# Query tiles of unequal width alternate in the self-attention sections of a two-block kernel

## What is computed

```python
QUERY_BLOCK = 128
def masked_probs(s, mask, sink=None):      # softmax over the keys that the mask leaves
    ...
def swa_mixer(q, k, v, pos, sinks):        # window of 128 keys: a block sees itself and the one before
    ...
def nsa_mixer(...):                        # compressed keys, selected blocks, window of 512
    ...
        return (g[..., 0:1] * o_cmp + g[..., 1:2] * o_sel + g[..., 2:3] * o_win)
def mla_mixer(...):                        # causal, scores are the sum of two products
        s = (jnp.einsum('bqhd,bkhd->bhqk', qn, k_nope)
             + jnp.einsum('bqhd,bkd->bhqk', qp, k_pe)).astype(jnp.float32) * scale
        p = masked_probs(s, kpos <= t)
        return jnp.einsum('bhqk,bkhd->bqhd', p.astype(v.dtype), v)
```

## Time and profile before

| | us |
|---|---|
| median of 3 runs | 3393.14 |
| the runs | 3391.33 to 3394.71 |
| the profiled execution | 3396.96 |
| its span (first to last instruction) | 3395.2 |
| PE busy in the span | 3277.1 (97%) |
| DVE busy | 1471.4 (43%) |
| ACT busy | 684.9 (20%) |
| section 0, 1, 2 of the first layer start near | 1136, 1309, 1555 |
| section 0, 1, 2 of the second layer start near | 2276, 2447, 2694 |

### The profile page before, as it was taken

How to read it: one execution, slowest core, us unless ns; L and a number is a source line. 1 busy time by engine, 2 the same in 40 slices (tenths; PEclk the granted TensorE clock), 3 DMA queues, 4 the chain that set the end, 5 groups by cost and what they waited for, 6 DMA issues and landing times.

```text
span 3395.2 us, 36971 instructions
## 1 busy us (share of the span) xinstructions
PE 3277.1 (97%) x14532; PEld 2105.3 (62%) x14532; DVE 1471.4 (43%) x2922; ACT 684.9 (20%) x1422; POOL 148.8 (4%) x106
## 2 busy tenths in 40 slices
PE   8999998999999999999999999999999999999998
PEld 3446345433433575765865888857467478568887
DVE  2352114212113646736644554346484375255533
ACT  2132111000002415413121000033361231210000
POOL 4400010000000100000000000000000000000000
PEclk9998998999999999999999999999999999999999
DMA  6110634999996121120221222221202112222221
GB/s 247 40 66 26 225 125 165 409 409 409 408 409 261 40 88 49 37 76 32 75 87 62 87 87 101 94 73 58 75 8 87 57 57 97 71 75 87 87 93 68
DMA packets 118635, 433.42 MB, mean 128 GB/s; under 512 B 13120, under 2 KB 13888, under 8 KB 117696
## 3 DMA queue, kind: packets, MB, share of 16 engines
q1 hardware_dynamic: 114768, 417.91, 33.0%
q10 hardware_dynamic: 3696, 13.16, 1.0%
HBM read 427.87 MB, written 3.15 MB: 127 GB/s over the span
## 4 chain that ended last, share of the span: by engine, by line
PE 85%; DVE 6%; DMA 4%; ACT 2%; issue 1%; DVEq 1%; POOL 0%; ACTq 0%; SPq 0%
PE bank L605 83%; DMA ring<-in_stream 2%; PE bank L1171 2%; DMA arena<-in_stream 2%; DVE arena L2088 1%; DVE arena L2113 1%; DVE arena L2110 1%; DVEq L2087 0%; ACT arena L1469 0%; DVE bank L2079 0%; ACT arena L1432 0%; DVE arena L2138 0%; DVE arena L2105 0%; DVE bank L2075 0%; ACT arena L1502 0%
## 5 line engine op out<-in xcount | busy, mean ns | idle before, releaser
L605 PE MATMUL bank<-arena 128*128 128x256 f32 (+14 forms) x5448 | 954.8, 389 | 36.3 <-ACT arena L1469 9.1
L605 PEld LDWEIGHTS bank<-arena 128*128 128x128 f32 (+4 forms) x5448 | 610.1, 173 | 324.8 <-issue 184.1
L605 PE MATMUL bank<-h,ring 128*128 128x256 f32 (+1 forms) x2000 | 672.8, 491 | 3.0 <-ACT rstd L1512 1.7
L605 PEld LDWEIGHTS bank<-h,ring 128*128 128x128 f32 x2000 | 384.2, 193 | 263.0 <-issue 230.8
L605 PE MATMUL bank<-arena,ring 128*128 128x256 f32 (+2 forms) x1888 | 513.5, 426 | 5.0 <-DVE y L1793 3.5
L605 PEld LDWEIGHTS bank<-arena,ring 128*128 128x128 f32 (+1 forms) x1888 | 336.8, 186 | 165.7 <-issue 122.4
L605 PE MATMUL bank<-ring,arena 128*64 128x512 f32 (+2 forms) x1184 | 282.7, 603 | 22.3 <-ACT arena L1315 11.5
L605 PE MATMUL bank<-y,ring 128*128 128x256 f32 (+1 forms) x800 | 253.9, 473 | 1.5 <-DVE y L1874 1.5
L605 PE MATMUL bank<-y,arena 128*128 128x256 f32 (+1 forms) x1032 | 231.8, 381 | 0.0
L1652 POOL TENSOR_TENSOR sq<-sq 128x512 f32<-128x512 f32 (+1 forms) x62 | 78.9, 1273 | 3179.8 <-ACT sq L1296 3179.8
L605 PEld LDWEIGHTS bank<-ring,arena 128*64 128x64 f32 (+2 forms) x1184 | 90.6, 139 | 203.9 <-issue 157.3
(11 more groups left out here) (299 smaller groups left out, 2445.1 us busy)
## 6 DMA issues: line engine op xcount, KB each, us to landing
ring<-in_stream SPq DMA_DIRECT2D x629, 512.0 KB, 4.6
arena<-in_stream SPq DMA_DIRECT2D x168, 512.0 KB, 12.8
x<-in_xT ACTq DMA_DIRECT2D x1, 2048.0 KB, 11.0
arena<-in_memT ACTq DMA_DIRECT2D x2, 1024.0 KB, 6.3
outT<-h ACTq DMA_DIRECT2D x8, 256.0 KB, 2.1
arena<-in_ctxT ACTq DMA_DIRECT2D x1, 1024.0 KB, 5.8
y<-in_inv ACTq DMA_DIRECT2D x1, 1024.0 KB, 4.8
memory_kv<-arena ACTq DMA_DIRECT2D x1, 1024.0 KB, 3.9
```

The lines of the kernel that those rows point to most:

```text
L605: ins = pe.matmul(out, lhsT, rhs, start=start, stop=stop, skip_group_check=loose)
```

## The change

Before the units get their numbers, the list is put in a new order for sections 0 to 2: first the units of qt 3 and qt 0 in turn (wide, narrow, wide, narrow, ...), then those of qt 2 and qt 1 in turn. The order inside a tile stays, and so do section 3 and all instructions of a unit. The number og of a tile follows the new order of completion: qt 3, 0, 2, 1. The two tiles that alternate have output banks 6 and 7.

```diff
@@ -523,9 +523,13 @@
+            def of(sec, qt):
+                return [u for u in out if u["sec"] == sec and u["qt"] == qt]
+            out = [u for sec in range(3) for wide, narrow in ((3, 0), (2, 1)) for two in zip(of(sec, wide), of(sec, narrow))
+                   for u in two] + [u for u in out if u["sec"] == 3]
             for i, u in enumerate(out):
                 u["n"] = i
-                u["og"] = 4 * u["sec"] + (TT - 1 - u["qt"] if u["sec"] < 3 else u["qt"])
+                u["og"] = 4 * u["sec"] + ((1, 3, 2, 0)[u["qt"]] if u["sec"] < 3 else u["qt"])
             return out
```

## The result

The changed kernel took 3429.45 us (median of four runs, 3422.01 to 3440.99) against 3392.68 us for the kernel before (3391.33 to 3394.71): a ratio of 1.0111, interval 1.0090 to 1.0133. The forecast was 3402 us with a range of 3396 to 3414. The direction is right, the size is not: 37 us were lost where 9 were forecast. Another thing is new. The four runs of the kernel before lie 3.4 us apart, those of the changed kernel 19.

The account below looks back on a forecast made before the run. PE was taken to bound wide units and DVE narrow ones, in a two-unit loop. Sections with drain +12.4, clock behind sections -6.5 and clock at starts +2.5 made +8.4 us: 3402 us, range 3396 to 3414.

Parts of the forecast that it names:

- What bounds the kernel, and the loop: PE bounds wide units, DVE narrow ones; a PE-DVE chain makes a (512, 128) pair 5.07 us instead of 4.66.
- Rival 1: Mixing works in the alternating sections: a pair takes only DVE's 4.37 us instead of 4.66, total 3376 us; chance 0.05.
- Section 1, +4.4: Section 1 of each layer: eight (512, 128) pairs lose 3.3 us, eight (384, 256) pairs 1.1, together 4.4.
- Section 0, +0.5: Section 0 of each layer: its first four pairs, widths 256 and 128, lose 0.14 us each, 0.5 together.
- Section 2, +1.3: Section 2 of each layer: 0.25 us for each of four pairs, 1.0, and 0.3 for the drain.
- 384, 256 stays bound by PE: 0: Section 2's pairs of 384 and 256 keys stay bound by PE and lose 0 us.
- Drain and the falls behind a section, -6.5: Section ends: last PV about 0.5 us later; half-clock falls behind five sections go, 1.3 us each, -6.5.
- The clock at a start: Section starts: with the second unit narrow, half clock may come or last longer; +2.5 us, bounds 0 and +15.
- rival 3: Half clock spreads at section starts, 20 us instead of 10, costing 3 to 5 us a place: 3407 to 3417; chance 0.20.
- Rival 2: Behind the sections, the ends stay slow and the five half-clock falls stay: 3408.5 us; chance 0.12.

Follow-up runs that it names:

- e8: Kernel before with only section 1 reordered, two wide units then two narrow ones in turn: 3414.86 us, ratio 1.0066.
- e16: The changed kernel run again with nothing altered, compared with the kernel before: 3419.18 us, ratio 1.0080.
- e13: Changed kernel with section 2 opening on two wide units (3 3 0 3 0 3 0 0), then tiles 2 and 1 in turn: 3404.90 us.
- e11: Kernel before with whole tiles from narrowest to widest (0, 1, 2, 3) in sections 0 to 2, no alternation: 3411.99 us, ratio 1.0053.
- e17: Kernel before with only section 2 reordered: 3 3 0 3 0 3 0 0, then tiles 2 and 1 in turn: 3394.40 us, ratio 1.0003.
- e15: Kernel before with only section 0 alternating, tiles 3 and 0, then 2 and 1: 3400.02 us, ratio 1.0018.

## Why the prediction was right or wrong

- **What bounds the kernel, and the loop** (right). The pair takes 5.07 us, term by term as added up. e8 gives the same reading with another order. Rival 1, the mix works, is out: 4.37 was its pair. The Trainium skill, Perfetto Trace Analysis, section Optimization Strategy, says that interleaving regimes with different bounds may improve performance; the premise held here and the result didn't: no order that mixed tiles was faster than whole tiles.
- **Section 1, +4.4** (nearly right). +5.8 and +5.2 in the first profile, +5.6 and +5.2 in e16. The (512, 128) pairs lose what was forecast, the (384, 256) pairs 0.04 each and not 0.14; the rest is for the most part at the section's start, 13.7 us at 0.50 where before had two falls of 3.4 in layer 1 and one of 10.2 in layer 2.
- **Section 0, +0.5** (too small). +1.1 to +1.6 in each layer in the changed kernel's profiles. Its first 10 to 14 us stand at half clock, where before had 10; how the rest divides I did not take apart.
- **Section 2, +1.3, and "384, 256 stays bound by PE: 0"**. With 3.4 us at half clock (e13) it took 50.04 and 49.82 us, 1.7 to 1.9 above the 48.14 of before in layer 2, though there the opening isn't the alternating one. The term was about right, in part by luck: the wide unit put at 4.2 us took 3.75 in the trace of before (transposes at 2705.05 and 2708.80), the narrow ones more than the 1.6 of the sum (up to 2.4). It is not what section 2 cost.
- **Drain and the falls behind a section, -6.5** (right). The way from a section's end to the next start got shorter by 1.1, 0.0, 1.7, 1.1, 0.8 and 1.2 us, 5.9 in all, the same to 0.1 us in every trace whose section ends with units of 384 and 256 keys in turn. The first product of the merge is at full clock behind both sections; before it was 3.63 us behind section 2. PE in the changed kernel:

```profile
1413.37 1.99 PE L609 MATMUL bank<-h,ring 128*128 128x256 f32 x8
...
1623.08 1.99 PE L609 MATMUL bank<-h,ring 128*128 128x256 f32 x8
```

  Rival 2, the ends stay slow, is out.
- **The clock at a start, "Bounds 0 and +15; I take +2.5"** (the step that failed). The mechanism was named, in this step and in rival 3, and its size was wrong. I took it that a fall lasts 10 us or perhaps 20, "3 to 5 for each place". In the changed kernel's four profiles it lasts 10 us at best and 61 at worst in section 2. All starts together stood at half clock for 47.8 us before, for 81.9 in e16 and for 126.3 in the first profile. The six sections grew by 22.6 and 48.9 us in these two, and chains and drains were to make 12.4 of that, so about 10 and 36 us stand where I put +2.5 (an estimate: the chains are not measured apart). I had read the narrowest stretch of section 1, which keeps 1.00, as evidence against rival 3. It shows that narrow units don't bring a full clock down; it says nothing of whether they bring a half clock up, and that was the question. e11 shows that in section 2 they don't, for over 20 us.
- **The scatter.** I priced one execution, as if the changed kernel would repeat like the one before. Its 22 executions spread over 32 us, 8 of them inside my range, and the four that made the result outside it; the medians of the three later sets are 3413 to 3419, so the 3429 of the result is from the upper part of the scatter. The 43.0 us of the first profile are e16's 16.5, 5.5 more ahead of section 0 and 21.3 more in layer 2's section 2; small differences in the other sections take back 0.4.
- **Rival 3** had the right place and 0.20; its own range, 3407 to 3417, ended below the 3429 too. The Trainium skill, TensorE: Matmul & The Clock Gate, section A second HAM failure mode, puts a swinging clock down to small idle gaps of PE between groups. The long stretch here doesn't swing, and has no gap in it: 61.20 of 61.20 us busy. The measurement decides; that rule describes something else than what happened.

Left open: what ends the half clock, and why the alternating opening holds it for so unequal a time; whether the moment of the fall is the whole difference between e13's sections 2 (3.4 us at 0.50) and e17's (6.8); and the 6 us of e15. No order tried here is faster than the kernel before.

## What to carry to other kernels

Two engines that take turns through small buffers form a loop, and mixing units of two sizes puts the heavy pieces of both into one way round it: add up that way before trusting the spare time of either engine. A stage whose start is met by the half clock should open with dense work, two such units next to each other, and put the sparse ones later, as section 2 did here; an order that opens thinly can cost more than the loop does, and from run to run a different amount. Where the clock may stay low for an unknown time, run the kernel often, and give the forecast that width.

## What the runs showed of the hardware

PE can stay at half clock for 61 us while the profile has it busy all the time, and in another execution of the same program return after 14 us, or stay for 34 us in the other layer. The 22 executions of that program lie 32 us apart (standard deviation 8.9), and the time at half clock follows their time at a correlation of 0.94; with a few neighbouring units of section 2 exchanged, seven executions (e13) lie 4.5 us apart (1.8). Half clock is not a factor of two in time either: a pair of section 2 went from 6.01 to 10.53 us, and 47.8 more microseconds at half clock cost 21.3, where 23.9 would be the price if PE alone set the pace. When whole tiles of 512 keys opened section 2, a fall that began 4.8 to 5.0 us behind the first scores lasted 10.2 us in seven cases, one at 5.3 us 3.4 in two. And the clock falls at places which no change touches: 13.7 us at 0.50 from 311 us on in one execution of the changed kernel, none there in the profiled one of before.
